# Dealing the next pass's k-projection out to the steps of an inversion and a recurrence, and moving r-projections to the pass's end

## The chip, the cores and the metric

One core of one Trainium2 chip. The metric is the device time of one execution in microseconds (us), as a median over runs. TensorE is called PE, its weight loads PEld, VectorE DVE, ScalarE ACT, GpSimd POOL, SyncE SP.

## What is computed

A decoder block on 1024 tokens (plus 16 prepended ones, TOK = 1040) of width 1024: RWKV-7 time mixing beside a short gated convolution, merged by gates, then a top-4-of-32 expert layer. The change is in the time mixing alone, cut to what matters here:

```python
proj = x_n @ w_in                      # r, k, v: columns 0:512, 512:1024, 1024:1536
r = pr + (shift(pr) - pr) * mu_r       # the same for k and v
w_log = -softplus(-(w0 + tanh(xw @ w_w1) @ w_w2)) - 0.5
a = sigmoid(a0 + (xa @ w_a1) @ w_a2);  g = sigmoid(xg @ w_g1) @ w_g2
kk = k * k_k / max(||k * k_k||, 1e-12) # norm per head of 64
k = k * (1 + (a - 1) * k_a)
S_t = S_{t-1} diag(w_t) + (S_{t-1} (-kk_t)) (kk_t a_t)^T + v_t k_t^T;  y_t = S_t r_t
yn = (y - mean(y)) / sqrt(var(y) + 64e-5) * lnx_g + lnx_b      # per head
out = ((yn + sum(r * k * r_k) * v) * g) @ w_o_rwkv
```

## The kernel before

Five engines run programs of their own, joined by semaphores. Each instruction that others wait for has a label in the list of its engine (PE_J, ACT_J, DVE_J, POOL_J, L213 to L252); `done(engine, label, j)` waits for it in pass j, `mark` sets it. An engine works strictly in the order written.

The channels of the time mixing are 512; a pass of the loop over `j` (NJ = 4) does 128 of them, two heads, for all tokens. Tokens stand in NCH = 4 chunks of CH = 260 for projections and in NC = 20 chunks of L = 52 for the recurrence. Weights of r, k, v for one pass stand in `ring` (slots 0, 1, 2), filled by SP (L354 to L360): k's next weights when `k_ps` says that the k-projection is through, r's and v's when their last chunk is.

A projection of one chunk (for k `project_keys`, L924) is eight products over the contraction, each of 128 x 128 weights and 260 columns in fp32; PE's records show two loads and two matmuls for each. ACT copies the chunk from PSUM to `pb` (`project_out`, L522).

The order of a pass on PE (L947 to L1119): products of the decay and of a (`z`, weights w2j); r chunks 0 and 1; the norm's sums (`n`, bones x nrm); r 2 and 3, v 0 to 3; transposes of b, k, a, v (L980); the products A (L983 to L995), which DVE masks into AT. Then the inversion of the triangular matrices: STEPS has 20 steps (five levels by four blocks), each with product P, a mask by DVE (P1), product D, an addition (Rw) and a transpose (Tw) by DVE (L1011 to L1029). In between stand products for X (`state_products`). Then xc, xb, m, nn (L1032 to L1062) and the first part of y. The recurrence (L1072 to L1078) takes the state S over 18 chunks: a product `s` with mxt, waited for by DVE, which makes the next S; behind each `s` PE does two products whose results nobody reads (bank 2 + h). Then u, yS and y. The pass's end: the bonus sums `bs` (bones x rkb), g (wg2j x lg), mean (bones x y_t), k chunk 0 of the next pass, var (bones x tmp), k chunks 1 to 3 (L1098 to L1119). The first k-projection stands before the loop (L929).

ACT in a pass (L520 to L592): evictions of k, Sigmoid for z and a, Square of kk (`sq`), three Exp (E1, E2, E0), evictions of r 0 and 1, Sqrt of the norm (`n`), the other evictions of r and v, then of everything from the transposes on; at the end the squares of the centred y (`ysq`) and their Sqrt (`var`). The compiler puts a table load ahead of a function of another table.

DVE in a pass (L699 to L830): k's shift and mix, 20 scans, csx, km, kmod, then nmax, the reciprocal and what hangs on kk; r's and v's mix; A's masks; the inversion's part; m, nn, the states S, u; then the bonus (`bo`), centring (`yc`), the reciprocal of var (`yrec`, L818), yn, yaff, ysum and yg. The last instruction (L830) sets `col_free`, on which PE, ACT and POOL wait at the next pass's head.

## Time and profile before

| | us |
|---|---|
| median of 3 runs | 2748.65 (2730.74 to 2750.43) |
| the profiled execution, its own time | 2747.56 |
| its span | 2746.0 |
| PE busy | 2569.7 (94%) |
| DVE busy | 1736.2 (63%) |
| ACT busy | 1279.0 (47%) |

Times are from the span's start. A busy PE is not PE at its peak: its clock has two levels, and the granted clock stands beside a stretch as a share (1.00 is 2.4 GHz, 0.50 is 1.2 GHz). "[3.40 <-issue]" means that the engine was idle for 3.40 us before and waited for nothing that the profile shows. A row of a stretch holds its bounds, its length, the busy time of PE, PEld, DVE, ACT and POOL with their instructions, the granted clock, the DMA share and GB/s. A row of a timeline holds start, duration, engine, line, operation, out<-in, the count merged, and the idle time before with what ended it. Passes of the mixing loop end at 240.64, 401.71, 550.84 and 698.47 us.

### The profile page before, as it was taken

To read this page: it belongs to the slowest core of one execution; us is meant where nothing else is said; L and a number is where in the kernel's file an instruction comes from. 1 tells how busy PE (TensorE), PEld (TensorE's weight loads), DVE (VectorE), ACT (ScalarE), POOL (GpSimd) and SP (SyncE) were. 2 spreads that over 40 slices of the span, in tenths; PEclk is the share of its full clock that TensorE was granted. 3 is DMA by queue.
4 is the path that set the end of the run, shared out by engine and by line. 5 is a ranking of instruction groups with operands and counts; after the bars stand their busy time and mean duration, and the time that the engine had idled before them with its cause. 6 is when DMAs were issued, how large, how long until landed. Compare 5 with 4: busy or idle time off the path is not lost.

```text
span 2746.0 us, 61801 instructions
## 1 busy us (share of the span) xinstructions
PE 2569.7 (94%) x24341; PEld 2194.8 (80%) x24341; DVE 1736.2 (63%) x2052; ACT 1279.0 (47%) x1379; POOL 514.4 (19%) x593
## 2 busy tenths in 40 slices
PE   7889988898898999998999999999999999999995
PEld 5677867777898999887787788888878888888884
DVE  8656547373422121254667677677679999999996
ACT  3303122131211111143566566666667777777776
POOL 6000000000000000113343342433421121111111
PEclk9988689898999999999999999999999999999997
DMA  5000000000011112155787787887889999999999
GB/s 125 16 3 18 10 11 18 2 25 3 24 46 46 46 46 69 59 131 88 272 294 277 264 295 268 288 295 272 286 317 392 379 377 380 383 384 381 379 380 341
DMA packets 143114, 527.87 MB, mean 192 GB/s; under 512 B 18412, under 2 KB 72272, under 8 KB 91011
## 3 DMA queue, kind: packets, MB, share of 16 engines
q1 hardware_dynamic: 120642, 480.00, 47.3%
q0 software_dynamic: 22336, 45.93, 6.9%
q8 instruction: 103, 1.69, 0.3%
q14 instruction: 33, 0.26, 0.0%
HBM read 492.01 MB, written 33.86 MB: 192 GB/s over the span
## 4 chain that ended last, share of the span: by engine, by line
PE 48%; DMA 3%; issue 1%; DVE 1%; ACT 0%; SPq 0%; POOLq 0%; POOL 0%; ACTq 0%; DVEq 0%
PE bank L2159 13%; PE bank L2160 13%; PE bank L2161 13%; PE bank L2168 5%; DMA raw_first<-in_w_e_up 2%; PE bank L2131 1%; PE bank L2200 1%; PE bank L2147 1%; PE bank L2232 1%; DVE h_fin L2038 0%; PE bank L2137 0%; PE bank L2174 0%; ACT w_hi L1734 0%; DMA x_rows<-hn_d,next_t 0%; DMA h_d<-y_rows,slot_t 0%
## 5 line engine op out<-in xcount | busy, mean ns | idle before, releaser
L1962 DVE TENSOR_TENSOR w_lo<-raw_first,w_hi 128x2048 fp32r<-128x2048 f32 x267 | 601.8, 2286 | 111.5 <-ACT w_hi L1734 111.4
L1734 ACT ACTIVATE w_hi<-raw_first 128x2048 fp32r<-128x2048 f32 x268 | 515.8, 1925 | 235.4 <-DMA raw_first<-in_w_e_up 89.3
L2159 PE MATMUL bank<-w_hi,x_hi 128*128 128x512 f32 x1056 | 421.1, 399 | 4.3 <-ACT yo_rows L1786 4.3
L2161 PE MATMUL bank<-w_hi,x_lo 128*128 128x512 f32 x1056 | 412.5, 391 | 0.0
L2160 PE MATMUL bank<-w_lo,x_hi 128*128 128x512 f32 x1056 | 412.1, 390 | 0.0
L1962 DVE TENSOR_TENSOR w_lo<-raw_rest,w_hi 128x2048 fp32r<-128x2048 f32 x132 | 299.0, 2284 | 2.9 <-ACT w_hi L1734 2.8
L1734 ACT ACTIVATE w_hi<-raw_rest 128x2048 fp32r<-128x2048 f32 x132 | 252.4, 1918 | 91.1 <-PE bank L2200 38.9
L913 PE MATMUL bank<-xm_hi,ring_hi 128*128 128x256 f32 (+1 forms) x896 | 260.9, 291 | 19.8 <-DVE dz L874 8.1
L913 PE MATMUL bank<-xm_hi,ring_lo 128*128 128x256 f32 (+1 forms) x896 | 254.6, 284 | 0.0
L913 PE MATMUL bank<-xm_lo,ring_hi 128*128 128x256 f32 (+1 forms) x896 | 253.5, 283 | 0.0
L2159 PEld LDWEIGHTS bank<-w_hi,x_hi 128*128 128x128 f32 x1056 | 199.2, 189 | 52.2 <-issue 12.8
L2161 PEld LDWEIGHTS bank<-w_hi,x_lo 128*128 128x128 f32 x1056 | 198.6, 188 | 42.6
L2160 PEld LDWEIGHTS bank<-w_lo,x_hi 128*128 128x128 f32 x1056 | 198.9, 188 | 38.9
L2159 PE MATMUL bank<-w_hi,a_hi 128*128 128x512 f32 x528 | 209.5, 397 | 0.0
L2160 PE MATMUL bank<-w_lo,a_hi 128*128 128x512 f32 x528 | 207.0, 392 | 0.0
L2161 PE MATMUL bank<-w_hi,a_lo 128*128 128x512 f32 x528 | 206.0, 390 | 0.0
L913 PE MATMUL bank<-xnT,ring 128*128 128x260 f32 x832 | 193.3, 394 | 3.2 <-ACT pb L523 2.0
L913 PEld LDWEIGHTS bank<-xm_hi,ring_hi 128*128 128x128 f32 x896 | 171.5, 191 | 22.5 <-DVE dz L874 8.3
L913 PEld LDWEIGHTS bank<-xnT,ring 128*128 128x128 f32 x832 | 162.9, 197 | 32.4 <-ACT pb L523 2.4
L882 DVE TENSOR_TENSOR gt<-gt,bank 128x256 f32<-128x256 f32 x64 | 24.1, 418 | 239.6 <-ACT gt L634 239.6
L913 PEld LDWEIGHTS bank<-xm_lo,ring_hi 128*128 128x128 f32 x896 | 171.2, 191 | 0.8
L913 PEld LDWEIGHTS bank<-xm_hi,ring_lo 128*128 128x128 f32 x896 | 170.8, 191 | 0.0
(381 smaller groups left out, 4300.9 us busy)
## 6 DMA issues: line engine op xcount, KB each, us to landing
raw_first<-in_w_e_up SPq DMA_DIRECT2D x134, 1024.0 KB, 7.0
raw_first<-in_w_e_gate SPq DMA_DIRECT2D x68, 1024.0 KB
raw_rest<-in_w_e_gate SPq DMA_DIRECT2D x68, 1024.0 KB
raw_first<-in_w_e_down SPq DMA_DIRECT2D x66, 1024.0 KB, 6.4
raw_rest<-in_w_e_down SPq DMA_DIRECT2D x66, 1024.0 KB
ring<-in_w_in SPq DMA_DIRECT2D x40, 512.0 KB, 4.0
h_all<-in_x SPq DMA_DIRECT2D x8, 512.0 KB, 15.1
hn_d<-hn SPq DMA_DIRECT2D x8, 512.0 KB
```

Source lines behind the costliest of these rows:

```text
L882: nc.vector.tensor_tensor(gt[:, b, m, :], gt[:, b, m, :], bank[4 * b + 2 + m][:, 0:256], ALU.mult).then_inc(gate_mul, 1)
L913: return nc.tensor.matmul(ps, lhsT, rhs, start=start, stop=stop)
L1734: nc.scalar.activation(w_hi[:, j % NRING, :, :], raw_piece(j), ACT.Copy).then_inc(hi_done, 1)
L1962: nc.vector.tensor_tensor(w_lo[:, j % NRING, :, :], raw_piece(j), w_hi[:, j % NRING, :, :].bitcast(f32), ALU.subtract).then_inc(lo_done, 1)
L2131: ins = nc.tensor.transpose(x_bank(f, wide)[:, k * 128:(k + 1) * 128], x_rows[:, c:c + 128], ident[:, :])
L2147: ins = nc.tensor.transpose(ta_ps[:, k * 128:(k + 1) * 128], u_t[:, k * 128:(k + 1) * 128], ident[:, :])
L2159: nc.tensor.matmul(ps[:, :], hi, w_hi[:, slot, k, :], start=start and k == 0, stop=False)
L2160: nc.tensor.matmul(ps[:, :], hi, w_lo[:, slot, k, :], start=False, stop=False)
L2161: ins = nc.tensor.matmul(ps[:, :], lo, w_hi[:, slot, k, :], start=False, stop=stop and k == HK - 1)
L2168: ins = nc.tensor.matmul(ps[OV * c:OV * (c + 1), 0:128], m[:, k0 + k, :], raw_piece(j)[:, k, 128 * c:128 * (c + 1)], start=start and k == ...
L2200: ins = nc.tensor.matmul(ps[:, :], kind_row[:, g % 2, :], bias_t[:, HC * h:HC * (h + 1)], start=False, stop=True)
L2232: nc.tensor.matmul(y_ps[n][:, :], kind_row[:, 2, :], bias_t[:, HC * n:HC * (n + 1)], start=True, stop=False)
```

## The change

- k's evictions go to a tile of their own, `pbk`, with counters `k_ev`, `r_ps`, `r_ev` of their own for what now crosses the pass's border.
- The k-projection of the next pass: products of chunks 0 and 1 stand one each behind steps 0 to 15 of the inversion (banks 6, 7), those of chunks 2 and 3 one each in chunks 1 to 16 of the recurrence (banks 3, 5), in place of the two products that nobody reads.
- PE gains a wait for k's evictions ahead of xb and one ahead of u.
- r chunks 0 to 2 of the next pass stand at the pass's end (and once before the loop); chunk 3 stays at the head, ahead of the norm's sums.
- At the pass's end the order is mean, bs, var, g, r; on DVE yc comes before bo.
- ACT does the norm's Sqrt before the three Exp, and tiny activations on `dz` make the tables of Sigmoid, Sqrt, Exp and Sqrt load ahead of the waits.

```diff
+    pbk = wk("pbk", [128, TOK + 2])
...
+    R_AHEAD = 3
+    K_BANK = (6, 7, 3, 5)
...
+        def keys_out(c, bk):
+            nc.scalar.activation(pbk[:, 2 + CH * c:2 + CH * (c + 1)], bank[bk][:, 0:CH], ACT.Copy).then_inc(k_ev, 1)
+
+        def receptance_out(c):
+            nc.scalar.activation(pb[:, 0, 2 + CH * c:2 + CH * (c + 1)], bank[4 + c % 2][:, 0:CH], ACT.Copy).then_inc(r_ev, 1)
+
+        def load_table(func, n):
+            nc.scalar.activation(dz[:, n:n + 1], eps_t[:, :], func)
+
+        for c in range(NCH):
+            act.wait_ge(k_ps, c + 1)
+            keys_out(c, 2 + c)
         for c in range(NCH):
             t = slice(CH * c, CH * (c + 1))
             act.wait_ge(lora_ps, 2 * c + 1)
@@ -517,15 +535,17 @@
             act.wait_ge(lora_ps, 2 * c + 2)
             nc.scalar.activation(lg[:, t], bank[6 + c % 2][:, 0:CH], ACT.Sigmoid).then_inc(lora_done, 1)
 
+        for c in range(R_AHEAD):
+            act.wait_ge(r_ps, c + 1)
+            receptance_out(c)
+
         with act.Fori(0, NJ) as j:
 
             def project_out(x, c, bk):
                 act_j.mark(nc.scalar.activation(pb[:, 'rkv'.index(x), 2 + CH * c:2 + CH * (c + 1)], bank[bk][:, 0:CH], ACT.Copy),
                            ('p', x, c))
 
-            for c in range(NCH):
-                act.wait_ge(k_ps, j * NCH + c + 1)
-                project_out('k', c, 2 + c)
+            load_table(ACT.Sigmoid, 4)
...
             act_j.mark(nc.scalar.activation(nrm[:, :], kk[:, :], ACT.Square), 'sq')
+            load_table(ACT.Sqrt, 5)
+            pe_j.done(act, ('n', NCH - 1), j)
+            for b in range(NCH):
+                act_j.mark(nc.scalar.activation(nrm[:, CH * b:CH * (b + 1)], bank[4 + b][:, 0:CH], ACT.Sqrt), ('n', b))
+            load_table(ACT.Exp, 6)
             dve_j.done(act, 'csx', j)
             act_j.mark(nc.scalar.activation(e1[:, :], cs[:, :], ACT.Exp, scale=-DECAY), 'E1')
             act_j.mark(nc.scalar.activation(e2[:, :], cs[:, :], ACT.Exp, scale=DECAY), 'E2')
             act_j.mark(nc.scalar.activation(e0[:, :], tmp[:, :], ACT.Exp, scale=-DECAY), 'E0')
-            for c in range(NCH):
-                if c == 2:
-                    pe_j.done(act, ('n', NCH - 1), j)
-                    for b in range(NCH):
-                        act_j.mark(nc.scalar.activation(nrm[:, CH * b:CH * (b + 1)], bank[4 + b][:, 0:CH], ACT.Sqrt), ('n', b))
-                pe_j.done(act, ('p', 'r', c), j)
-                project_out('r', c, c % 2)
+            pe_j.done(act, ('p', 'r', 3), j)
+            project_out('r', 3, 1)
...
+            dve_j.done(act, 'k', j)
+            for c in range(2):
+                act.wait_ge(k_ps, j * NCH + NCH + c + 1)
+                keys_out(c, K_BANK[c])
...
+            for c in range(2, NCH):
+                act.wait_ge(k_ps, j * NCH + NCH + c + 1)
+                keys_out(c, K_BANK[c])
...
+            load_table(ACT.Sqrt, 7)
             for c in range(NCH):
                 pe_j.done(act, ('var', c), j)
-                act_j.mark(nc.scalar.activation(nrm[:, CH * c:CH * (c + 1)], bank[4 + c % 2][:, 0:CH], ACT.Sqrt,
+                act_j.mark(nc.scalar.activation(nrm[:, CH * c:CH * (c + 1)], bank[2 + c % 2][:, 0:CH], ACT.Sqrt,
                                                 bias=epsx_t[:, :], scale=1.0 / HS), ('var', c))
+            for c in range(R_AHEAD):
+                act.wait_ge(r_ps, j * R_AHEAD + R_AHEAD + c + 1)
+                receptance_out(c)
...
+        def keys_part(c, k, bk):
+            ins = mm(bank[bk][:, 0:CH], ring[:, 1, k, :], xnT[:, k, CH * c:CH * (c + 1)], k == 0, k == KT - 1)
+            if k == KT - 1:
+                ins.then_inc(k_ps, 1)
+
+        def project_receptance(c):
             for k in range(KT):
-                ins = mm(bank[2 + c][:, 0:CH], ring[:, 1, k, :], xnT[:, k, CH * c:CH * (c + 1)], k == 0, k == KT - 1)
-            ins.then_inc(k_ps, 1)
+                ins = mm(bank[4 + c % 2][:, 0:CH], ring[:, 0, k, :], xnT[:, k, CH * c:CH * (c + 1)], k == 0, k == KT - 1)
+            ins.then_inc(r_ps, 1)
...
+        pe.wait_ge(ring_in[0], 16)
+        pe.wait_ge(k_ev, NCH)
+        for c in range(R_AHEAD):
+            if c >= 2:
+                pe.wait_ge(r_ev, c - 1)
+            project_receptance(c)
...
-            for q in range(2 * NCH):
-                x, c = 'rv'[q // NCH], q % NCH
-                if c == 0:
-                    pe.wait_ge(ring_in['rkv'.index(x)], j * 16 + 16)
-                if q < 2:
-                    act_j.done(pe, ('z', 2 + c), j)
-                else:
-                    act_j.done(pe, ('p', 'rv'[(q - 2) // NCH], (q - 2) % NCH), j)
+            act_j.done(pe, ('z', 3), j)
+            for k in range(KT):
+                ins = mm(bank[1][:, 0:CH], ring[:, 0, k, :], xnT[:, k, CH * 3:CH * 4], k == 0, k == KT - 1)
+            pe_j.mark(ins, ('p', 'r', 3))
+            act_j.done(pe, 'sq', j)
+            for b in range(NCH):
+                pe_j.mark(mm(bank[4 + b][:, 0:CH], bones[:, :], nrm[:, CH * b:CH * (b + 1)]), ('n', b))
+            pe.wait_ge(ring_in[2], j * 16 + 16)
+            for c in range(NCH):
+                if c == 1:
+                    act_j.done(pe, ('p', 'r', 3), j)
+                if c >= 2:
+                    act_j.done(pe, ('p', 'v', c - 2), j)
                 for k in range(KT):
-                    ins = mm(bank[c % 2][:, 0:CH], ring[:, 'rkv'.index(x), k, :], xnT[:, k, CH * c:CH * (c + 1)], k == 0, k == KT - 1)
-                pe_j.mark(ins, ('p', x, c))
-                if q == 1:
-                    act_j.done(pe, 'sq', j)
-                    for b in range(NCH):
-                        pe_j.mark(mm(bank[4 + b][:, 0:CH], bones[:, :], nrm[:, CH * b:CH * (b + 1)]), ('n', b))
+                    ins = mm(bank[c % 2][:, 0:CH], ring[:, 2, k, :], xnT[:, k, CH * c:CH * (c + 1)], k == 0, k == KT - 1)
+                pe_j.mark(ins, ('p', 'v', c))
...
+                if i == 0:
+                    pe.wait_ge(ring_in[1], j * 16 + 32)
+                if i < 2 * KT:
+                    keys_part(i // KT, i % KT, K_BANK[i // KT])
...
+            pe.wait_ge(k_ev, j * NCH + NCH + 2)
+            pe.sem_inc(pe_passed, 1)
...
-                for h in range(2):
-                    mm(bank[2 + h][hp(h), 0:2 * L], mxt[hp(h), c, :], ar[hp(h), :, c, 0:L])
+                if c <= 2 * KT:
+                    keys_part(2 + (c - 1) // KT, (c - 1) % KT, K_BANK[2 + (c - 1) // KT])
             dve_j.done(pe, ('S', NC - 2), j, pe_passed)
+            pe.wait_ge(k_ev, j * NCH + 2 * NCH)
+            pe.sem_inc(pe_passed, 1)
...
-                pe_j.mark(mm(bank[2 + c][:, 0:CH], bones[:, :], rkb[:, CH * c:CH * (c + 1)]), ('bs', c))
-            act_j.done(pe, ('y', 1, 1), j)
+                act_j.done(pe, ('y', c // 2, 1), j)
+                pe_j.mark(mm(bank[2 + c][:, 0:CH], bones[:, :], y_t[:, CH * c:CH * (c + 1)]), ('mean', c))
             for c in range(NCH):
-                pe_j.mark(mm(bank[(0, 1, 6, 7)[c]][:, 0:CH], wg2j[:, :], lg[:, CH * c:CH * (c + 1)]), ('g', c))
+                pe_j.mark(mm(bank[(0, 1, 6, 7)[c]][:, 0:CH], bones[:, :], rkb[:, CH * c:CH * (c + 1)]), ('bs', c))
+            for c in range(NCH):
+                act_j.done(pe, ('ysq', c), j)
+                if c >= 2:
+                    act_j.done(pe, ('var', c - 2), j)
+                pe_j.mark(mm(bank[2 + c % 2][:, 0:CH], bones[:, :], tmp[:, CH * c:CH * (c + 1)]), ('var', c))
             for c in range(NCH):
                 dve_j.done(pe, ('bo', c), j)
-                pe_j.mark(mm(bank[2 + c][:, 0:CH], bones[:, :], y_t[:, CH * c:CH * (c + 1)]), ('mean', c))
-            pe.wait_ge(ring_in[1], j * 16 + 32)
-            dve_j.done(pe, ('yc', 0), j)
-            project_keys(0)
-            for c in range(NCH):
-                act_j.done(pe, ('ysq', c), j)
-                if c == 0:
-                    dve_j.done(pe, ('yc', NCH - 1), j)
+                pe_j.mark(mm(bank[(0, 1, 6, 7)[c]][:, 0:CH], wg2j[:, :], lg[:, CH * c:CH * (c + 1)]), ('g', c))
+            pe.wait_ge(ring_in[0], j * 16 + 32)
+            for c in range(R_AHEAD):
                 if c >= 2:
-                    act_j.done(pe, ('var', c - 2), j)
-                pe_j.mark(mm(bank[4 + c % 2][:, 0:CH], bones[:, :], tmp[:, CH * c:CH * (c + 1)]), ('var', c))
-            project_keys(1)
-            for c in (2, 3):
-                act_j.done(pe, ('var', c), j)
-                project_keys(c)
+                    pe.wait_ge(r_ev, j * R_AHEAD + R_AHEAD + c - 1)
+                project_receptance(c)
```

## Rows read from the trace of the kernel before

**Rows 1.** Busy time by stretch: pass 2 and pass 4.

```profile
240.64:401.71 161.07, 146.99 (x2192) 129.39 (x2192) 88.11 (x161) 34.72 (x68) 6.91 (x13) 0.78 0.04 12
...
550.84:698.47 147.63, 130.33 (x2192) 110.56 (x2192) 85.94 (x161) 31.84 (x63) 6.91 (x13) 0.90 0.04 12
```

**Rows 2.** Busy time by stretch: inversion, passes 1, 2, 4.

```profile
139.28:172.22 32.94, 27.89 (x881) 26.84 (x881) 25.17 (x61) 1.58 (x3) 3.51 (x5) 1.00 0.01 4
...
290.00:336.87 46.87, 45.66 (x881) 45.42 (x881) 27.26 (x61) 1.58 (x3) 3.51 (x5) 0.53 0.01 3
...
600.41:632.98 32.57, 27.77 (x881) 26.73 (x881) 25.10 (x61) 1.58 (x3) 3.51 (x5) 1.00 0.01 4
```

**Rows 3.** Timeline of DVE, pass 1, then passes 3 and 4.

```profile
106.59 0.70 DVE L732 TENSOR_SCALAR nrm<-nrm 128x1040 f32<-128x1040 f32 x1 [6.80 <-ACT nrm L547]
...
539.16 6.65 DVE L818 RECIPROCAL nrm<-nrm 128x1040 f32<-128x1040 f32 x1 [5.74 <-ACT nrm L591]
...
554.30 0.06 DVE L700 MEMSET pb<- 128x6 f32 x1 [3.40 <-issue]
...
563.12 1.24 DVE L694 SCALAR_TENSOR_TENSOR k_t<-pb,k_t 128x1040 f32<-128x1040 f32 x1
...
568.56 0.70 DVE L732 TENSOR_SCALAR nrm<-nrm 128x1040 f32<-128x1040 f32 x1 [4.20 <-ACT nrm L547]
...
587.92 1.24 DVE L691 TENSOR_TENSOR v_t<-pb 128x1040 f32<-128x1040 f32 x1 [0.69 <-ACT pb L523]
...
589.20 1.30 DVE L694 SCALAR_TENSOR_TENSOR v_t<-v_t,vj,pb 128x1040 f32<-128x1040 f32 x1
```

**Rows 4.** Timeline of ACT, end of pass 3 and head of pass 4.

```profile
526.87 1.35 ACT L583 ACTIVATE y_t<-bank 128x260 f32<-128x260 f32 x4 [34.54 <-PE bank L913]
...
532.14 1.73 ACT L588 ACTIVATE tmp<-y_t 128x260 f32<-128x260 f32 x4 [3.92 <-DVE y_t L694]
...
536.94 0.92 ACT L591 ACTIVATE nrm<-bank,epsx_t 128x260 f32<-128x260 f32 x2 [3.06 <-PE bank L913]
...
558.01 1.07 ACT L538 ACTIVATE nrm<-kk 128x1040 f32<-128x1040 f32 x1 [1.35 <-DVE kk L717]
...
566.01 1.28 ACT L547 ACT_TABLE_LOAD   x1
...
567.30 1.22 ACT L547 ACTIVATE nrm<-bank 128x260 f32<-128x260 f32 x4
```

**Rows 5.** Timeline of PE, end of pass 3 and head of pass 4.

```profile
526.01 1.49 PE L913 MATMUL bank<-AT,U 52*64 52x52 f32 x80 [0.40 <-PE bank L913]
...
527.43 2.02 PE L913 MATMUL bank<-rkb,bones 128*128 128x260 f32 x8
...
536.30 2.31 PE L913 MATMUL bank<-tmp,bones 128*128 128x260 f32 x8
...
538.45 10.68 PE L913 MATMUL bank<-xnT,ring 128*128 128x260 f32 x48
...
592.74 1.09 PE L980 MATMUL bank<-ident,v_t 128*128 128x128 f32 x8
...
594.45 0.41 PE L913 MATMUL bank<-ar,bh 64*64 64x104 f32 x8
```

**Rows 6.** Timeline of PE, one step of the inversion in pass 4.

```profile
614.29 0.79 PE L913 MATMUL bank<-Tw,AT 52*64 52x52 f32 x20 [0.44 <-issue]
...
615.49 0.75 PE L913 MATMUL bank<-Tw,AT 52*64 52x52 f32 x20
```

**Rows 7.** Timeline of DVE, the state S in the recurrence of pass 1.

```profile
195.96 0.28 DVE L694 SCALAR_TENSOR_TENSOR S<-bank,pc,np__57 128x64 f32<-128x64 f32 x1 [0.52 <-PE bank L913]
...
199.49 0.28 DVE L694 SCALAR_TENSOR_TENSOR S<-bank,pc,np__57 128x64 f32<-128x64 f32 x1 [0.66 <-PE bank L913]
```

**Rows 8.** Busy time by stretch, recurrence to bonus sums: pass 2, all four.

```profile
355.06:378.30 23.24, 18.26 (x398) 14.21 (x388) 6.89 (x22) 0.58 (x2) 0.00 (x0) 0.78 0.01 2
...
sum 98.35, PE 81.63 PEld 62.48 DVE 27.46 ACT 2.26 POOL 0.00; mean PE 20.41 PEld 15.62 DVE 6.86 ACT 0.57 POOL 0.00
```

More of the change, by code:

```diff
@@ L212, in mixing_program @@
     Y_BANK = ((0, 1), (6, 7))
-    PE_J = ([('z', c) for c in range(NCH)] + [('p', 'r', 0), ('p', 'r', 1)] + [('n', c) for c in range(NCH)]
-            + [('p', 'r', 2), ('p', 'r', 3)] + [('p', 'v', c) for c in range(NCH)] + [('t', x, g) for x in TA for g in range(3)]
+    PE_J = ([('z', c) for c in range(NCH)] + [('p', 'r', 3)] + [('n', c) for c in range(NCH)]
+            + [('p', 'v', c) for c in range(NCH)] + [('t', x, g) for x in TA for g in range(3)]
             + [('A', g) for g in range(NP)])
@@ L227, in mixing_program @@
              + [('u', g) for g in range(2)] + ['yS'] + [('y', g) for g in range(2)]
-             + [('bs', c) for c in range(NCH)] + [('g', c) for c in range(NCH)]
-             + [('mean', c) for c in range(NCH)] + [('var', c) for c in range(NCH)])
-    ACT_J = ([('p', 'k', c) for c in range(NCH)] + [(x, c) for c in range(NCH) for x in 'za'] + ['sq', 'E1', 'E2', 'E0', ('p', 'r', 0), ('p', 'r', 1)]
-             + [('n', c) for c in range(NCH)] + [('p', 'r', 2), ('p', 'r', 3), ('p', 'v', 0), ('p', 'v', 1)]
-             + [('p', 'v', 2), ('p', 'v', 3)] + [('t', x, g) for x in TA for g in range(3)]
+             + [('mean', c) for c in range(NCH)] + [('bs', c) for c in range(NCH)]
+             + [('var', c) for c in range(NCH)] + [('g', c) for c in range(NCH)])
+    ACT_J = ([(x, c) for c in range(NCH) for x in 'za'] + ['sq'] + [('n', c) for c in range(NCH)] + ['E1', 'E2', 'E0', ('p', 'r', 3)]
+             + [('p', 'v', c) for c in range(NCH)] + [('t', x, g) for x in TA for g in range(3)]
              + [('xa', g) for g in range(3)]
@@ L249, in mixing_program @@
               + ['S0'] + [('S', c) for c in range(NC - 1)]
-              + [('u', g, h) for g in range(2) for h in range(2)] + [('bo', c) for c in range(NCH)]
-              + [('yc', c) for c in range(NCH)] + ['yrec', 'yn', 'yaff', 'ysum'] + [('yg', c) for c in range(NCH)])
+              + [('u', g, h) for g in range(2) for h in range(2)] + [('yc', c) for c in range(NCH)]
+              + [('bo', c) for c in range(NCH)] + ['yrec', 'yn', 'yaff', 'ysum'] + [('yg', c) for c in range(NCH)])
     POOL_J = ['w2', 'wg2', 'vj', 'pads', 'cols'] + [(x, b) for b in range(NB) for x in ('M0', 'R0')]
@@ L316, in mixing_program @@
     k_ps = sem("k_ps")
+    k_ev = sem("k_ev")
+    r_ps = sem("r_ps")
+    r_ev = sem("r_ev")
     pbz = sem("pbz")
@@ L705, in shift_mix @@
                 i = 'rkv'.index(x)
-                act_j.done(dve, ('p', x, NCH - 1), j)
-                old, new = pb[:, i, 1:TOK + 1], pb[:, i, 2:TOK + 2]
+                if x == 'k':
+                    dve.wait_ge(k_ev, j * NCH + NCH)
+                    old, new = pbk[:, 1:TOK + 1], pbk[:, 2:TOK + 2]
+                else:
+                    act_j.done(dve, ('p', x, NCH - 1), j)
+                    old, new = pb[:, i, 1:TOK + 1], pb[:, i, 2:TOK + 2]
                 if x == 'v':
@@ L810, in on_vector @@
             for c in range(NCH):
-                pe_j.done(dve, ('bs', c), j)
-                tt(('bo', c), chunks(kk[:, CH * c:CH * (c + 1)]), chunks(bank[2 + c][:, 0:CH]), v_t[:, 5 * c:5 * c + 5, 0:L], ALU.mult)
-            for c in range(NCH):
                 pe_j.done(dve, ('mean', c), j)
@@ L816, in on_vector @@
                     ALU.mult, ALU.add)
+            for c in range(NCH):
+                pe_j.done(dve, ('bs', c), j)
+                tt(('bo', c), chunks(kk[:, CH * c:CH * (c + 1)]), chunks(bank[(0, 1, 6, 7)[c]][:, 0:CH]), v_t[:, 5 * c:5 * c + 5, 0:L],
+                   ALU.mult)
             act_j.done(dve, ('var', NCH - 1), j)
@@ L954, in on_tensor @@
                 pe_j.mark(mm(bank[6 + c % 2][:, 0:CH], w2j[64:128, :], lw[64:128, CH * c:CH * (c + 1)]), ('z', c))
[L955 to L969 removed]
+            act_j.done(pe, ('z', 3), j)
+            for k in range(KT):
+                ins = mm(bank[1][:, 0:CH], ring[:, 0, k, :], xnT[:, k, CH * 3:CH * 4], k == 0, k == KT - 1)
[9 more added lines that the diff above has]
+                    act_j.done(pe, ('p', 'v', c - 2), j)
+                for k in range(KT):
+                    ins = mm(bank[c % 2][:, 0:CH], ring[:, 2, k, :], xnT[:, k, CH * c:CH * (c + 1)], k == 0, k == KT - 1)
+                pe_j.mark(ins, ('p', 'v', c))
             dve_j.done(pe, 'bh', j)
```

6 lines of the change are left out of this document (3 added, 3 removed).

## The prediction

> **What bounds the kernel now.** I read the stretches by pass first. Four passes of the mixing loop (128 channels each) fill 88 to 698 us of the 2746; the pass length is set inside the pass, since the transfers are at a few per cent there, and the change touches nothing behind 698 us. Pass 4 takes 147.63 us (pass 3 1.5 more), pass 2 takes 161.07 [rows 1]. The stretches inside a pass say why: the inversion lasts 32.94 us in pass 1 and 32.57 in pass 4 (pass 3 is like them) at full granted clock, and 46.87 in pass 2, where the clock stands at the lower level (1.2 GHz) nearly throughout and PE is busy 45.66 of it [rows 2]. Everything else in a pass is a relay of chains.
>
> The timelines of DVE, ACT and PE around the seam between passes 3 and 4 show who is late where. At a pass's end the tail is: the y products, their evictions, mean, centring, squares, variance, Sqrt, then DVE's reciprocal. DVE waits 5.74 us for the last Sqrt [rows 3], ACT had done the squares by 533.87 and took up the first variance at 536.94 [rows 4], because PE does the row sums of the bonus, the gates' product and one chunk of k-projection in between: PE order is bones x rkb at 527.43, variance at 536.30 [rows 5]. From the reciprocal to the end of the pass DVE is alone (539.16 to 550.84, 11.7 us), and PE does the other three chunks of k-projection under it: hidden. At the next pass's head DVE itself bounds (3.40 us without a releaser at its loop's head, then shift, scans, kmod to 564.36); then it waits 4.20 us for the norm's Sqrt [rows 3], which waits on ACT behind three Exp, two r evictions and a table load of 1.28 us [rows 4]. From there PE's six further chunks of r and v (6 x 3.5 us) and DVE's chain (568.56 to 590.50) run side by side, and PE's transposes end where the A products start, at 594.45, 43.6 us into the pass [rows 3, 5].
>
> **The change part by part.** The sum is made against the profiled execution, 2747.56 us (span 2746.0), 1 us under the median of 2748.65.
>
> 1. *Head of a pass.* PE now has one chunk of r before the norm's sums instead of two, and ACT does Sqrt before Exp, with both table loads issued ahead of the wait. One chunk is 16 records, 8 products: 24 products take 10.68 us [rows 5], so 0.445 each and 3.5 a chunk. New timing, from the pass's start at 0: z as before, sq ends at 8.24; r3 about 6 to 9.5; norm sums to 11.3; the four Sqrt (1.22 [rows 4]) end at 12.6. DVE's kmod ends at 13.5 (563.12+1.24-550.84), so the 4.2 us wait goes and DVE is the late one. DVE's chain then runs without a hole to v, whose 0.7 us wait for its eviction also goes: v ends at 34.8 instead of 39.66. v-projection: chunk 0 to about 15, then PE must wait until ACT has done Exp x3 and evicted r3 (17.5), three more chunks end at 28.3: ahead of DVE's need at 32.2. The transposes of v take 592.74 to 594.45 = 1.7. So A starts at about 36.7, not 43.6: **-6.9 in passes 2, 3 and 4**. The ends: 0 if the loop's head stalls PE or ACT as DVE's does (3.40 us), since both now finish their pass at the same moment as DVE, not 2 us before it; 6.9 if the slack of 1 us before kmod covers it. I keep 6.9 and put 0.5 a pass for that risk below. In pass 1 three chunks of r stand before the loop, 10.5 us on the path; they are out of the stretch before the norm again (2 chunks, 7.0) and the later slack of the v evictions gives back the other 3.5; DVE waited 6.80 us in that place [rows 3]. I take 0 there, bounds -2 and +4.
>
> 2. *Inversion.* 16 products of k are dealt to its steps: 16 x 0.445 = 7.1 us of PE. A step costs PE 1.20 us at full clock (614.29 to 615.49 [rows 6]), and PE is not at work in 4.8 of the 32.57 us: some of it in holes named issue, 0.44 us before that step, one every three or four steps [rows 2, 6]. At half clock, where PE draws half as many instructions a microsecond, the holes are gone (1.2 us idle of 46.87 [rows 2]), so I read them as instructions arriving late, and four longer instructions a step let them arrive. Floor 7.1-4.8 = +2.3, ceiling +7.1 if no hole closes, and twice that, 14, if each change from 64-row tiles to the whole array costs as much as a product (no row shows it). I take **+3 a pass**, nearest the floor: +9 for passes 1, 3, 4. For pass 2 see the clock. The two added waits of PE for ACT's evictions (banks 6, 7 before xb, banks 3, 5 before u) stand behind products finished five steps, or two, earlier, while ACT is idle: nothing.
>
> 3. *The clock.* In pass 2 the clock fell while PE still had holes, just after A, and then stayed down through 43 us of work in which PE shows 97% busy with tiles of 52 x 64. The other three inversions did the same work at full clock. I take it that one such product in each step keeps or brings the clock back: pass 2's inversion becomes 36 us like the others, **-10.9**. If it does not, a product costs 0.89, and the same stretch becomes 46.87+14.2 = 61. The Trainium skill (TensorE: Matmul & The Clock Gate, "What's actually happening") says that a busy engine releases the throttle. By that rule busy time is what counts; the row of pass 2 disagrees, as 45.66 of 46.87 us busy did not release it [rows 2].
>
> 4. *Recurrence to the end of y.* The two idle products of a step (removed) make room for one k product. Full-clock step: the state's product to DVE's result is 0.52+0.28 = 0.80 us; half clock 0.66+0.28 = 0.94 [rows 7]. k's 0.445 behind the state's product fits in 0.80. At half clock 0.89 and about 0.24 for the state's own product (estimate: its four records of 64 columns against k's two of 260) are 1.13, over 0.94: +0.19 x 16 = +3.0 a pass. Now the clock is down for much of it: the four stretches from the recurrence to the bonus sums are 98.35 us together, and even the best, of pass 2, is 23.24 at a mean clock of 0.78 [rows 8]. With the k products I expect full clock: 18 x 0.80 plus 0.8 of start, and about 7.4 for the two groups of products behind it, 22.6 a pass, 90.4 in four: **-7.9**; ends +12 (clock down, four passes) and -8.
>
> 5. *Tail.* mean comes first, waits for the eviction of its half of y; bonus sums after it; variance directly after; g behind it. From y's start (526.01) evictions end at 2.2 [rows 4], means start at 1.6 and 2.5, the centring ends at 4.1, squares at 4.6 (0.46 behind, as before). Then ACT loads Sqrt's table on the path: 1.28 + 0.3 for the tiny activation (estimate, a quarter of 1.22) = 6.2. Variances 0 and 1 are there at 5.8, and from first Sqrt to reciprocal is 2.2 as now. Reciprocal at 8.4 instead of 13.15: **-4.75 in each of four passes = -19.0**. Bounds: 3.2 a pass if the table load costs double, 6.3 if it costs nothing. The three r chunks follow g at 9.3 and end at 19.8; the pass ends at 20.1 by DVE: just hidden. After pass 4 they are idle work, and ACT's last eviction delays the next stage by 0.4.
>
> 6. *Small:* +0.4 there, and 0.5 x 3 at the loop's heads: +1.9. SP's code is unchanged; its load of k for the pass after next is released earlier, and r's at 9.5 us of a pass, 100 us ahead of need.
>
> Sum: -20.7 +9 -10.9 -7.9 -19.0 +1.9 = **-47.6, so 2700.0 us.**
>
> **The rivals.**
> A. *The clock stays down in one inversion, as now.* For: PE will be idle 1.6 us more before v's transposes (DVE now last), right before the place where it fell in pass 2. Against: k products. Price: 61 instead of 36 for that pass: -47.6+25 = -22.6, **2725**. [...]
> B. *The recurrence stays at half clock* and its step grows to 1.13: -7.9 becomes about +10, **2718**.
> C. *The head gives nothing*, because PE or ACT, now ending with DVE, meet a hole of 3.4 us at the loop's head and the load of Sigmoid's table behind it: z ends later than DVE's scans want it, 2 to 3 us a pass, +8: **2708**. The Trainium skill (Runtime: NRT & Kernel Launch, "Instruction fetch mechanics") says a taken branch out of the fetched window stalls for a fetch; DVE's 3.40 us agrees.
> D. *Slower.* Longer idleness before A brings every inversion to half clock, with k in it: passes 1, 3, 4 at 61 instead of 36, pass 2 at 61: -47.6+4 x 25 = +52, **2800**. It decides from two such passes on (+2.4, no gain). For: pass 2. Against: three of four inversions held although the holes were there, and k fills them.
> E. *Products cost 14 in the inversion* (the change of tiles): +11 a pass, 4 passes: -4, **2744**, no difference.
>
> **How the numbers follow.** Forecast with its own spread (2690 to 2715, C inside it) 0.56; A 0.19; B 0.12; E 0.07; D 0.06. A measurement tells 1% (27 us, 2721) from no change. Faster by over 1%: forecast, B, and a third of A: 0.74; within 1%: the rest of A, and E: 0.20; slower: D, 0.06. The range leaves out D and most of E, and reaches past A: 2684 (no hole left, table load hidden) to 2732.
>
> **What would show it.** DVE's wait for the norm's Sqrt gone, and for the variance's Sqrt near 2 us; A's first product 37 us into passes 2 to 4; inversions of 35 to 37 us at full clock with 0.44 us products inside and fewer holes; recurrence steps of 0.80 us at full clock; passes 2 to 4 at 137 to 140 us. Wrong if an inversion reads 45 or more, if a recurrence step reads 1.1, or if PE ends its r chunks behind DVE's last product.

## The result: less than half of the gain that was forecast, and the profile after

| | before | after |
|---|---|---|
| median of 20 runs each, us | 2744.86 | 2724.08 |
| lowest and highest | 2723.28, 2774.57 | 2712.78, 2749.01 |
| the profiled execution: its own time, span | 2747.56, 2746.0 | 2712.78, 2711.2 |

The ratio is 0.9945 with a 95% interval of 0.9919 to 0.9971. By the medians the change saves 21 us, by the ratio 15, where the forecast was 48. The profiled execution after is the quickest of its 20, and the one before had an inversion at half clock, so these two differ by 34.8 us, more than the medians do. Both facts matter below.

Busy time by stretch, the changed kernel: its four passes, then the four inversions, then the four recurrences.

```profile
86.01:241.86 155.85, 138.30 (x2168) 111.24 (x2168) 87.61 (x160) 35.72 (x74) 6.74 (x12) 0.96 0.04 12
241.86:385.12 143.26, 126.14 (x2121) 101.22 (x2120) 87.40 (x161) 35.05 (x72) 6.93 (x13) 0.96 0.05 13
385.12:527.32 142.20, 125.05 (x2121) 100.03 (x2120) 87.42 (x162) 35.05 (x72) 6.93 (x13) 0.98 0.05 14
527.32:668.39 141.07, 124.94 (x2121) 100.10 (x2120) 87.39 (x161) 35.05 (x72) 6.93 (x13) 0.98 0.04 10
...
139.93:179.07 39.14, 38.49 (x912) 31.92 (x913) 26.93 (x61) 2.36 (x5) 3.53 (x5) 1.00 0.01 3
283.57:322.71 39.14, 38.49 (x912) 31.92 (x913) 26.93 (x61) 2.35 (x5) 3.52 (x5) 1.00 0.01 3
...
569.04:608.42 39.38, 38.74 (x913) 32.10 (x913) 26.93 (x61) 2.35 (x5) 3.52 (x5) 1.00 0.01 3
...
197.93:214.16 16.23, 15.04 (x119) 8.33 (x110) 5.11 (x18) 0.78 (x2) 0.00 (x0) 1.00 0.01 4
...
626.82:643.05 16.23, 15.04 (x118) 8.33 (x110) 5.11 (x18) 0.78 (x2) 0.00 (x0) 1.00 0.00 1
```

Pass 4 is 6.6 us shorter than in [rows 1]. Inside it an inversion is 6.8 us *longer* than in [rows 2]: PE is busy 38.74 us instead of 27.77, and its idleness has shrunk from 4.8 us to 0.64. All four stand at full clock.

Timeline of DVE, the end of pass 3 and the head of pass 4.

```profile
515.63 6.65 DVE L855 RECIPROCAL nrm<-nrm 128x1040 f32<-128x1040 f32 x1 [2.34 <-ACT nrm L619]
...
529.70 0.06 DVE L732 MEMSET pb<- 128x6 f32 x1 [2.32 <-issue]
...
538.52 1.24 DVE L726 SCALAR_TENSOR_TENSOR k_t<-pb,k_t 128x1040 f32<-128x1040 f32 x1
539.68 0.70 DVE L768 TENSOR_SCALAR nrm<-nrm 128x1040 f32<-128x1040 f32 x1
...
558.27 1.23 DVE L723 TENSOR_TENSOR v_t<-pb 128x1040 f32<-128x1040 f32 x1
```

The waits of 5.74, 4.20 and 0.69 us of [rows 3] have become 2.34, nothing and nothing, and the hole at the loop's head 2.32 instead of 3.40.

Timelines of ACT and PE around the same seam.

```profile
510.26 1.75 ACT L615 ACTIVATE tmp<-y_t 128x260 f32<-128x260 f32 x4 [0.41 <-DVE y_t L726]
512.03 1.28 ACT L525 ACT_TABLE_LOAD   x1
513.32 0.20 ACT L525 ACTIVATE dz<-eps_t 128x1 f32<-128x1 f32 x1
513.43 0.83 ACT L619 ACTIVATE nrm<-bank,epsx_t 128x260 f32<-128x260 f32 x2
...
527.40 0.39 ACT L522 ACTIVATE pb<-bank 128x260 f32<-128x260 f32 x1 [3.12 <-PE bank L950]
527.80 1.28 ACT L525 ACT_TABLE_LOAD   x1
```

```profile
512.66 1.04 PE L950 MATMUL bank<-tmp,bones 128*128 128x260 f32 x4
...
516.68 10.68 PE L950 MATMUL bank<-xnT,ring 128*128 128x260 f32 x48
```

The variance starts 5.4 us behind y's first product (at 507.24) instead of 10.3 [rows 5]. The table load is all but hidden: Sqrt starts at 513.43, and the variance's first chunk ended at 513.27, since PE did the bonus sums until 512.66. The three r chunks end (527.4) just as DVE ends the pass (527.32).

The two profiled executions by parts, their sums over the four passes in us:

| part | before | after | difference | forecast |
|---|---|---|---|---|
| pass's start to A, passes 2 to 4 | 130.55 | 107.29 | -23.3 | -20.7, +1.5 for the loop's heads |
| pass 1 up to A, with its earlier start | | | +0.65 | 0 |
| inversions | 145.34 | 157.04 | +11.7 | -1.9 |
| xc to the recurrence | 72.87 | 74.50 | +1.6 | 0 |
| recurrence to the first row sums | 98.35 | 97.53 | -0.8 | -7.9 |
| row sums to the variance's reciprocal | 47.5 | 27.5 | -20.0 | -19.0 |
| behind the loop | 2047.5 | 2042.8 | -4.7 | +0.4 |

Counted from y's first product, as the forecast counted its tail, the four come to 35.45 us instead of 53.97: -18.5. The last row isn't shown to be the change's: in three other executions that stretch took 2050.6 us (the kernel before), 2045.2 and 2048.4 (the changed one).

### The profile page after: what moved, and what is told of

It is laid out like the page before. It is cut to its first block, busy times and chain, and to the rows that moved or that the text cites. A ratio compares the mean times of both kernels' runs of the same rounds, so it can differ in the third digit from the quotient of the medians.

```text
span 2711.2 us, 61346 instructions
## 1 busy us (share of the span) xinstructions
PE 2543.1 (94%) x24101; PEld 2144.0 (79%) x24101; DVE 1740.4 (64%) x2053; ACT 1284.2 (47%) x1402; POOL 519.6 (19%) x593
## 4 chain that ended last, share of the span: by engine, by line
PE 49%; DMA 3%; issue 1%; DVE 1%; ACT 0%; SPq 0%; POOLq 0%; POOL 0%; ACTq 0%; DVEq 0%
PE bank L2213 13%; PE bank L2214 13%; PE bank L2215 13%; PE bank L2222 5%; DMA raw_first<-in_w_e_up 2%; PE bank L2185 1%; PE bank L2254 1%; PE bank L2201 1%; PE bank L2286 1%; DVE h_fin L2092 0%; PE bank L2191 0%; PE bank L2228 0%; ACT w_hi L1788 0%; DMA h_d<-y_rows,slot_t 0%; DMA next_t<-slot_d 0%
## 5 line engine op out<-in xcount | busy, mean ns | idle before, releaser
L950 PE MATMUL bank<-xnT,ring 128*128 128x260 f32 x880 | 241.6, 413 | 13.9 <-ACT pb L545 9.9
```

The source lines that it names most:

```text
L950: return nc.tensor.matmul(ps, lhsT, rhs, start=start, stop=stop)
```

## The experiments

**The inversion of pass 2, by chance or by rule?** The kernel before once more, unchanged.

> The kernel before, unchanged, for a second profile. Theory (the half-clock inversion of pass 2 was a chance of that one execution): four inversions of 33 us each at clock 1.00, the mixing loop 12 to 14 us shorter than the 610.8 us (87.7 to 698.5) of the first profile. Rival (it falls in every execution): again one inversion of about 47 us at clock near 0.5.

It took 2732.4 us with a span of 2730.8. Busy time by stretch, its inversion of pass 2 and its recurrences of passes 1 and 2:

```profile
285.63:318.17 32.54, 27.76 (x880) 26.73 (x881) 25.21 (x61) 1.58 (x3) 3.52 (x5) 1.00 0.02 4
...
187.99:205.09 17.10, 15.01 (x153) 9.82 (x150) 5.12 (x18) 0.00 (x0) 0.00 (x0) 0.50 0.00 1
334.82:352.01 17.19, 13.38 (x144) 8.78 (x145) 5.11 (x18) 0.00 (x0) 0.00 (x0) 0.63 0.00 1
```

No inversion is at half clock (32.0 to 32.6 us, all four at 1.00): whether one falls differs from one execution to the next, and one that does costs 14 us. The recurrences stood wholly or mostly at half clock and took 17.1 to 17.2 us, 1.6 more than the best of the first profile (15.52 in pass 2, at a mean of 0.81): the two unread products of a step fit beside the chain.

**What a product costs in a step.** One lone 128 x 128 x 260 product was added to the kernel *before*, read by nobody, behind each of the first 16 steps. Nothing else of the change is in it.

```diff
+                if i < 2 * KT:
+                    mm(bank[6][:, 0:CH], bones[:, :], xnT[:, i % KT, 0:CH])
```

> The kernel before with one product of 128 x 128 weights and 260 columns (bones x normed tokens, result read by nobody) behind each of steps 0 to 15 of the inversion, nothing else moved. Theory (a lone whole-array product between 64-row tiles costs 0.77 us of PE, of which the holes of the kernel before hide about 6 of 12 us): each inversion 39.1 us, steps 1.94 us apart, clock 1.00. Rival (the product costs 0.445 as in a block, and the rest comes from the order of the changed kernel): 35 to 36 us.

Its time was 2772.9 us (span 2771.3). The inversions, passes 1 and 2:

```profile
139.47:178.86 39.39, 38.70 (x912) 32.05 (x913) 26.92 (x61) 1.58 (x3) 3.51 (x5) 1.00 0.01 3
293.60:332.74 39.14, 38.49 (x912) 31.92 (x913) 26.92 (x61) 1.58 (x3) 3.51 (x5) 1.00 0.01 3
```

All four took 39.14 to 39.39 us, the changed kernel's 39.14 to 39.38, so the whole of the inversion's loss is that of the dealt products. (Against the kernel profiled again the whole run lost 13 us beyond its inversions. Most of that, 3 us in each of passes 2 to 4, lies behind the recurrence, where y's products stood at half clock: 28.1 us from the recurrence's start to the first row sums instead of 24.5 to 25.2.) One step of the changed kernel, timeline of PE:

```profile
582.49 0.79 PE L950 MATMUL bank<-Tw,AT 52*64 52x52 f32 x20
583.11 0.75 PE L950 MATMUL bank<-Rw,P 52*64 52x52 f32 x20
583.79 0.71 PE L950 MATMUL bank<-xnT,ring 128*128 128x260 f32 x2
584.43 0.79 PE L950 MATMUL bank<-Tw,AT 52*64 52x52 f32 x20
```

From start to start, P takes 0.62, D 0.68 and the product 0.64: 1.94 us a step where it was 1.17 between holes (615.49 to 616.66 in the timeline before). The product thus costs 0.77, of which 0.64 is its own slot and 0.13 is added to its neighbours, against 0.445 in a block [rows 5]. That is a plain step; over a whole inversion, set against pass 2 of the kernel profiled again, PE is busy for 10.7 us more, so 0.67 a product in the mean, and idle for 4.1 less: +6.6.

Where the holes were, in the timeline of PE before, pass 4:

```profile
605.96 0.56 PE L913 MATMUL bank<-Tw,AT 52*64 52x52 f32 x13 [0.43 <-issue]
...
610.14 0.79 PE L913 MATMUL bank<-Tw,AT 52*64 52x52 f32 x20 [0.47 <-DVE Rw L691]
...
616.66 0.75 PE L913 MATMUL bank<-Tw,AT 52*64 52x52 f32 x20
```

Behind the first step, PE has 238 to 242 records of products and loads between one hole (0.12 to 0.76 us) and the next, here and in the kernel profiled again, also where the view names DVE. The holes go by the count of instructions and not by the step, which bears out the reading that instructions arrive late. They stood 3.8 to 4.7 us apart in pass 4; in the changed kernel's inversion the same count takes 5.1 us in the mean, and none above 0.05 us is left. The 0.6 us that stay idle there are a wait for DVE behind the last step.

**Fewer changes between the two kinds of tiles.** The 16 products two at a time (behind every second step), and four at a time.

```diff
-                if i < 2 * KT:
-                    keys_part(i // KT, i % KT, K_BANK[i // KT])
+                if i < 2 * KT and i % 2 == 1:
+                    for p in range(i - 1, i + 1):
+                        keys_part(p // KT, p % KT, K_BANK[p // KT])
```

> The changed kernel with the 16 products of the inversion issued two at a time, behind every second step. Theory (the extra 0.33 us is paid at each entry into whole-array work, not per product): 8 entries fewer, 2.6 us less, inversion 36.5 us. Rival (each product costs 0.77 here wherever it stands): 39.1 us as in the changed kernel.

> The changed kernel with the 16 products issued four at a time, behind steps 3, 7, 11 and 15. Theory (price per entry): 4 x (0.77 + 3 x 0.445) = 8.4 us of PE instead of 12.3, inversion 35.2 us at clock 1.00, a whole run some 15 us under the changed kernel. Rival (price per product): 39.1 us. A third possibility: blocks of 2.1 us leave DVE without work and the holes of PE come back between them, then 36 to 38 us.

The fours stand behind steps 3, 7, 11 and 15. Pairs: 2715.7 us, inversions 37.23, 37.39, 37.23 and 37.23. Fours: a median of 2728.4 us over 4 runs, ratio 0.9897 (0.9816 to 0.9978), inversions 37.04 to 37.79. The slot of a pair is 1.08 us, that of a four 1.95; timelines of PE, pairs and fours:

```profile
591.75 1.15 PE L950 MATMUL bank<-xnT,ring 128*128 128x260 f32 x4
592.83 0.79 PE L950 MATMUL bank<-Tw,AT 52*64 52x52 f32 x20
```

```profile
591.08 2.02 PE L950 MATMUL bank<-xnT,ring 128*128 128x260 f32 x8
593.03 0.79 PE L950 MATMUL bank<-Tw,AT 52*64 52x52 f32 x20
```

Slots of 0.64, 1.08 and 1.95 us are 0.20 plus 0.44 a product, so the extra price is one of the change of tile, paid once a group. Pairs win 1.9 us a pass. Their idle time is 1.26 us, but no hole named issue has returned: 0.60 of it is PE's wait for DVE behind step 0, where no product stands now, and 0.61 the wait at the end. Fours win no more than pairs, since with them 0.5 to 1.1 us of such holes are back (idle 1.7 to 2.3). What these runs brought unasked is their recurrences, here of pairs, passes 1 and 2:

```profile
191.57:207.80 16.23, 15.04 (x118) 8.33 (x110) 5.11 (x18) 0.78 (x2) 0.00 (x0) 1.00 0.02 5
328.75:355.27 26.52, 25.33 (x119) 12.93 (x110) 5.11 (x18) 0.78 (x2) 0.00 (x0) 0.52 0.02 6
```

The same 16 products at half clock take 26.5 us instead of 16.2. That is rival B's mechanism at more than three times its price.

**Does the changed kernel do that too?** Itself, once more.

> The changed kernel, unchanged, for a second profile. Theory (the recurrence with a k product in each step has two states, 16.2 us at clock 1.00 or 26.5 to 27.3 at 0.50, and a run's time counts how many of its four are in the lower one): inversions 39.1 to 39.4 at clock 1.00; the time is 2711 to 2714 plus 10 to 11 per recurrence at half clock. Rival (the recurrence of the changed kernel is always at full clock and the spread of its times comes from behind 668 us): four recurrences of 16.2 whatever the time.

It took 2734.4 us (span 2732.8), with the recurrence of pass 1 at half clock (27.28 us). Stretches of that pass from the inversion's end on, then two steps in the timelines of PE and DVE:

```profile
180.97:184.00 3.03, 1.37 (x77) 1.25 (x78) 0.00 (x0) 0.67 (x2) 0.00 (x0) 1.00 0.02 5
184.00:190.00 6.00, 5.70 (x55) 5.70 (x56) 0.00 (x0) 1.91 (x5) 0.00 (x0) 0.51 0.01 3
190.00:200.00 10.00, 7.20 (x326) 6.61 (x323) 3.69 (x10) 1.74 (x3) 0.00 (x0) 0.95 0.01 3
200.00:202.00 2.00, 1.32 (x31) 1.15 (x31) 0.28 (x1) 0.00 (x0) 0.00 (x0) 0.79 0.00 0
202.00:228.36 26.36, 25.17 (x100) 12.51 (x99) 4.82 (x17) 0.78 (x2) 0.00 (x0) 0.50 0.02 5
```

```profile
209.32 1.23 PE L950 MATMUL bank<-xnT,ring 128*128 128x260 f32 x2
210.48 0.48 PE L950 MATMUL bank<-S,mxt 64*64 64x64 f32 x4
210.89 1.23 PE L950 MATMUL bank<-xnT,ring 128*128 128x260 f32 x2
...
209.44 0.28 DVE L726 SCALAR_TENSOR_TENSOR S<-bank,pc,np__57 128x64 f32<-128x64 f32 x1 [1.29 <-PE bank L950]
```

The same at full clock, timeline of PE, pass 4 of the first profile:

```profile
635.81 0.33 PE L950 MATMUL bank<-S,mxt 64*64 64x64 f32 x4
636.07 0.71 PE L950 MATMUL bank<-xnT,ring 128*128 128x260 f32 x2
636.71 0.33 PE L950 MATMUL bank<-S,mxt 64*64 64x64 f32 x4
```

A step is 1.57 us; it was 0.90 at full clock. The k product's slot is 1.16 (209.32 to 210.48) against 0.64, and the state's own 0.41 against 0.26. Both lie on one chain, since the k product is longer than DVE's answer and the next state's product waits behind it on PE. (Rival B had 0.89 and 0.24 for the two.) Before the change half clock showed only as DVE's wait of 0.66 instead of 0.52 [rows 7].

Whether the clock is down is settled at the recurrence's start: with a k product a step, all 28 stood either at 1.00 throughout or at 0.50 to 0.53. Here it had dipped in the ten microseconds after xc and come back, then fell within 2 us of the first state's product. PE then worked 25.17 of 26.36 us, on 128-row products among them, and the level stayed at 0.50. In the changed kernel's third profile, told of below, the recurrence of pass 3 fell with no such dip (16.14 us at 1.00 ahead of it). Why one falls and the next does not stays open.

The same profile shows a second thing that the quickest execution hid, at the head. Timelines of DVE and PE, pass 4:

```profile
557.96 0.70 DVE L768 TENSOR_SCALAR nrm<-nrm 128x1040 f32<-128x1040 f32 x1 [0.66 <-ACT nrm L562]
...
549.60 5.31 PE L950 MATMUL bank<-xnT,ring 128*128 128x260 f32 x16 [0.58 <-ACT sg L553]
```

The r chunk ahead of the norm's sums took 5.2 to 5.3 us from its start to the sums' (3.6 in the first profile), with a granted clock of 0.83 in the first 10 us of the pass, and DVE waited for the norm's Sqrt again. So A came at 37.3 to 37.45 us in passes 2 to 4, and at 37.3 to 37.4 in two of three in the third profile: 1.6 us later than in the first.

**Is the dealing needed at all?** Without it: the k-projection of 32 products as one block at the pass's end, all four r chunks at the head, the two unread products back in the recurrence, and the rest of the change as it is (order at the pass's end, Sqrt ahead of Exp, early table loads).

```diff
-                if i < 2 * KT:
-                    keys_part(i // KT, i % KT, K_BANK[i // KT])
...
-            pe.wait_ge(ring_in[0], j * 16 + 32)
-            for c in range(R_AHEAD):
-                if c >= 2:
-                    pe.wait_ge(r_ev, j * R_AHEAD + R_AHEAD + c - 1)
-                project_receptance(c)
+            pe.wait_ge(ring_in[1], j * 16 + 32)
+            for c in range(NCH):
+                if c == 2:
+                    act_j.done(pe, ('var', 3), j)
+                for k in range(KT):
+                    keys_part(c, k, K_BANK[c])
```

> The changed kernel without the dealing: k's products as one block of 32 at the pass's end behind g, the two unread products back in the recurrence, all four r chunks at the head (one before the norm's sums, three behind); the order of the tail, of ACT and the table loads stay as changed. Theory: inversion back to 32 to 33 us, recurrence 15.5 to 17.2; norm's wait gone but A is not earlier (seven chunks of r and v behind the norm's sums), head 43 to 44; reciprocal of the variance 8.4 us behind y's start, but the k block ends 3 us behind DVE, so the pass gains 1.5 to 2 us of the 4.75. Per pass 3 to 6 us more than the changed kernel at full clock (146 against 142), and some 2735 in all. Rival (dealing costs more than it buys): 2720 or less.

The median was 2772.9 us over 9 runs, ratio 1.0091 (1.0057 to 1.0126): slower than before. The tail kept its gain (6.58 to 6.60 us from row sums to reciprocal in all four passes), but the heads of passes 2 to 4 came to 52.4 to 53.4 us. Timelines of DVE and PE at the head of pass 3:

```profile
402.01 1.24 DVE L712 TENSOR_TENSOR k_t<-pbk 128x1040 f32<-128x1040 f32 x1 [1.59 <-ACT pbk L518]
...
417.53 0.70 DVE L757 TENSOR_SCALAR nrm<-nrm 128x1040 f32<-128x1040 f32 x1 [5.68 <-ACT nrm L557]
...
401.66 1.14 PE L939 MATMUL bank<-lw,w2j 64*128 64x260 f32 x6
...
407.82 6.66 PE L939 MATMUL bank<-xnT,ring 128*128 128x260 f32 x16 [0.65 <-ACT sg L548]
```

With 14 us of k behind the variance PE comes 3.6 us late to the new pass (401.66, where DVE had ended the old one at 398.06); the r chunk, at a clock of 0.55, takes 6.66 us, and DVE waits for both. So the tail's gain is kept here and lost again at the next head. With 14 us of projection dealt away, heads and tails both win, and the inversion's 6.6 us a pass is what that costs. This one arrangement also moved the r chunks back to the head; the two were not told apart. My 43 to 44 us for these heads missed the late start. Two of the four inversions here (47.14 and 47.97 us) are at half clock again, about 30 us of this execution's time; without them it would stand near 2743, still above the 2732 of the kernel before profiled again (an estimate).

**Paying less in the inversion.** Chunk 0 of k as a block behind the first chunk of v at the head, chunk 1 as four pairs behind steps 3, 7, 11 and 15, chunks 2 and 3 in the recurrence as in the changed kernel.

```diff
+                    pe.wait_ge(ring_in[1], j * 16 + 32)
+                    for k in range(KT):
+                        keys_part(0, k, K_BANK[0])
...
-                if i < 2 * KT:
-                    keys_part(i // KT, i % KT, K_BANK[i // KT])
+                if i % 4 == 3 and i < 16:
+                    for k in range(i // 2 - 1, i // 2 + 1):
+                        keys_part(1, k, K_BANK[1])
```

> The changed kernel with k's chunk 0 as a block behind v's first chunk at the head (where PE waits 2.5 us for an eviction) and chunk 1 as four pairs behind steps 3, 7, 11 and 15; chunks 2 and 3 in the recurrence as changed. Theory: inversion 34.5 us (four entries of 1.2 us, mostly in holes), head 35.8 to 36.6, so 4 us a pass less than the changed kernel and 16 us in all, near 2708 median, with the two states of the recurrence as before. Rival (the head is bound by PE as closely as by DVE): head 38 to 39, and the gain is 4 to 8 us.

Median 2716.8 us over 4 runs, ratio 0.988 (0.982 to 0.994). Inversions took 33.9 to 35.7 us and the heads of passes 2 to 4 36.4 to 37.6, where the changed kernel has 35.8 to 37.45: the chunk at the head was nearly free, and the four pairs cost 1 to 3 us. Yet two recurrences of the profiled execution took 27.63 us.

The next takes the products out of most of the recurrence: chunk 2 is a block just before it, chunk 3 stands in its steps 1 to 8.

```diff
+            for k in range(KT):
+                keys_part(2, k, K_BANK[2])
...
-                if c <= 2 * KT:
-                    keys_part(2 + (c - 1) // KT, (c - 1) % KT, K_BANK[2 + (c - 1) // KT])
+                if c <= KT:
+                    keys_part(3, c - 1, K_BANK[3])
```

> As n1, but k's chunk 2 is a block of eight products just ahead of the recurrence and chunk 3 goes into its steps 1 to 8; steps 9 to 18 have only the state's product. Theory (what is before the recurrence decides its clock, and a block of whole-array work holds it up): recurrences at clock 1.00 in at least the first steps, 15.4 us plus 3.6 for the block, no stretch of 26 us. Rival (the recurrence itself is too thin to hold the clock, wherever it starts): it falls inside the recurrence, and the eight products of chunk 3 cost 0.6 us more each, 20 to 21 us plus the block.

Median 2721.4 us over 9 runs, ratio 0.9903 (0.9868 to 0.9939). All four recurrences took 16.02 or 16.03 us at a mean clock of 0.86 or 0.87, and none came near 27. The block in front costs most of what it saves: xc to the recurrence took 22.4 to 25.0 us instead of 18.3 to 19.9. One inversion here took 37.5 us at a mean clock of 0.95; the others took 34.4 to 35.9.

**Is that arrangement really better than the changed kernel?** Both once more, on one chip, beside the same runs of the kernel before.

> The arrangement of n1 again (chunk 0 of k as a block at the head, chunk 1 as pairs behind steps 3, 7, 11 and 15 of the inversion, chunks 2 and 3 in the recurrence), timed beside the changed kernel on one chip. Theory (the price of a product alone between the 64-row tiles is what the dealing loses; it does not depend on the chip): inversions of 34 to 36 us against 39.1, the median 5 to 10 us below the changed kernel's, ratio to the kernel before 0.986 to 0.992. Rival (n1's gain over the changed kernel was the luck of four runs; the dealing of chunks 2 and 3 puts the recurrence at half clock just as often, at 10 to 11 us each): medians of the two within 4 us.

> The changed kernel itself, timed beside n1_repeat on the same chip. Theory: ratio to the kernel before 0.993 to 0.997 as in its first timing, a median of 2720 to 2730; inversions 39.1 to 39.4 at full clock; each of the four recurrences either 16.2 us at full clock or about 27 at half, so that single times stand some 11 us apart by their number. Rival (half-clock recurrences belong to one chip's or one hour's state): no recurrence at half clock here and a median near 2713.

Over 12 runs each, the new arrangement came to 2732.0 us, ratio 0.9941 (0.9905 to 0.9977), the changed kernel to 2724.6, ratio 0.9911 (0.9877 to 0.9945), the kernel before to 2746.0 over 23. The first's 0.988 over four runs did not come again (the two intervals overlap), and the theory that it would be 5 to 10 us quicker than the changed kernel found no support: its median is 7 us above. Its inversions did take 34.8 to 36.5 us, 15 us less in four than the changed kernel's; its recurrences of passes 2 and 4 took it back:

```profile
332.97:360.59 27.62, 26.28 (x115) 13.46 (x111) 5.10 (x18) 0.78 (x2) 0.00 (x0) 0.50 0.03 8
...
623.22:650.87 27.65, 26.29 (x116) 13.46 (x111) 5.10 (x18) 0.78 (x2) 0.00 (x0) 0.50 0.00 1
```

The changed kernel had one such recurrence here (26.20 us, pass 3). The two arrangements' intervals overlap; none that I tried is shown to be better than the change itself.

Over all profiled executions, the granted clock in the two places (the arrangement with the block is left out of the recurrences, as its steps hold half the products):

| | at half clock | of |
|---|---|---|
| inversions without dealt products | 3 | 12 |
| inversions with dealt products (the lowest at 0.95) | 0 | 36 |
| recurrences with a k product a step, the changed kernel | 2 | 12 |
| the same, in pairs, fours and chunk 0 at the head (twice) | 8 | 16 |

## Why the prediction was wrong

**Step 1, the head: right, to a little more.** The norm's Sqrt ends at 11.6 us of the pass, DVE has no hole up to v, and A starts at 35.8 us instead of 36.7 (forecast -20.7, measured -23.3). That is the first profile; in five of the six heads of the other two it came at 37.3 to 37.45, so that the mean of all nine, 36.7, is the forecast's. Rival C is refuted: Sigmoid's table load stands at the pass's head (527.80), but DVE needs z only for its scans at 533.3. Its own hole in that place was smaller too. The Trainium skill (Runtime: NRT & Kernel Launch, "Instruction fetch mechanics") has a taken branch whose target isn't in the fetched window stall for a fetch; the hole of 2.32 us at the loop's head agrees, though no run shows that it is a fetch. Pass 1 came out near the 0 forecast (+0.65): DVE's wait of 6.80 us became 4.31 there, and behind the three r chunks ahead of the loop it waited 9.27 us for z.

**Step 2, the inversion: the step that failed.** I forecast +3 a pass "nearest the floor", with a product at its price in a block and holes that hide most of it. The measured price is +6.6, because a lone product between 64-row tiles costs 0.77 in a plain step and 0.67 in the mean, and not 0.445: the term of 7.1 us of PE work measured 10.7. The holes did close, for 4.1 us, as my +3 implied: the mechanism held and the price was off. (At half clock PE had 19 product records a microsecond and not half of the 27 at full clock, as I had put it; the reading of the holes stands without that.) With pass 2 counted like the others the forecast term was 4 x 3 = 12 and the measured one 26, so 14 us are lost here. The ceiling I gave, +7.1, holds the value; rival E (+14) had the right mechanism at twice its size, as it took the change for a whole product and no hole for closed. The kernel before with unread products shows this without anything else of the change.

**Step 3, the clock in the inversion: fits, but isn't shown.** With products in the steps none of 36 was at half clock, without them 3 of 12; two of those three are of the undealt kernel, and for the kernel before it is 1 of 8. What I had taken from one execution (-10.9) is a matter of chance for the kernel before: the one profiled again had none and took 2732.4 us. Rivals A and D came in no inversion.

**Step 4, the recurrence: wrong twice.** At full clock a step is 0.90 and not 0.80 us, because k's product holds PE for 0.64 and not 0.445, the same error as in step 2: 16.23 us at best, against 15.5 to 17.5 before. The -7.9 came to -0.8 even in the best execution: 4.1 of the 7.1 us are the recurrences (64.9 in four instead of 60.8), and 3.0 the products behind them (32.6 instead of 29.6). And at half clock the step is 1.57 us, where rival B said 1.13: 10 to 11 us for one recurrence instead of 3. I gave B a chance of 0.12 as a thing of all four; it comes singly. With 2 of 12, an execution of the changed kernel has 0.7 of them, or 7 us in the mean. With the later heads (some 3 us in the mean of the three profiles) that is the likely reason that the median stands 11 us above the first profiled execution, the only one of the three that had no such recurrence. I had expected 128-row products to keep the clock up here as in the inversion: they don't. The Trainium skill (TensorE: Matmul & The Clock Gate, "What's actually happening") says that activity releases the throttle; 25.17 us busy of 26.36 at a clock of 0.50 disagree, as the row of pass 2 did before.

**Step 5, the tail: right, with a wrong bound.** -20.0 for -19.0. The table load took 1.28 us and the tiny activation 0.1 (0.20 long, with the next one 0.11 behind its start) instead of 0.3, but only some 0.13 us of both lay on the path, as the variance itself wasn't there earlier. So the bound of 6.3 a pass for a load that costs nothing could not be reached. The r chunks end with the pass, as said.

The first two profiles differ by 34.8 us where 47.6 were forecast. The inversions lost 13.6 us against the forecast, the recurrences with what follows 7.1, xc to the recurrence 1.6 and pass 1 0.7; the heads gave 4.1 more than forecast, the tails 1.0, and 5.1 came behind the loop, which may be chance. The medians, 20.8 us apart, take off 14 more: the 11 told of in step 4, and 3 since the first profile of the kernel before was that much slower than its median.

Part of the gain against that profile is luck, for it had the inversion at half clock. Against the kernel before profiled again, which had none, the changed kernel's first profile has a mixing loop 11.8 us shorter (582.4 for 594.2): heads -23.5, tails -19.4, inversions +27.8, the rest +3.3. Head and tail carry all the gain that is left.
